# Two transformer blocks on one core: the order of weight halves, of the last differential head, of retention's sums and of the mixing sums

## The reference

```python
# first block
xn = rms_norm(h, g0);  proj = xn @ w_in          # q, k, v, forget gate, q, k, v, two gates
o_a = forgetting_attention(...)                   # 8 heads of 64
o_b = stick_breaking_attention(...)               # 8 heads of 64
mixed = (sigmoid(g_a) * (o_a @ w_o_fox) + sigmoid(g_b) * (o_b @ w_o_sb)) @ w_out
h = h + rms_norm(mixed, g1)
u = causal_depthwise_conv(rms_norm(h, g2) @ w_up) # width 2 x 2816, taps 3
h = h + rms_norm((gelu(u_gate) * u_val) @ w_down, g3)
# second block
proj = rms_norm_2(x, g_mix) @ w_in                # qa, ka, va, qr, kr, vr, gr, gate_a, gate_r
ya = rms_norm_2(diff_attention(qa, ka, va, lam), g_diff_sub) * 0.8     # 8 heads
yr = silu(gr) * rms_norm_2(retention(qr, kr, vr), g_ret_sub)           # 4 heads, two chunks of 128
x = x + (sigmoid(gate_a) * (ya @ w_branch_diff) + sigmoid(gate_r) * (yr @ w_branch_ret)) @ w_out
x = x + square(relu(rms_norm_2(x, g_mlp) @ w_ff1)) @ w_ff2
x = x + sigmoid(rms_norm_2(x, g_ple) @ w_ple_gate) * (p @ w_ple)
out = rms_norm_2(x, g_final)
```

## Time and profile before

| | us |
|---|---|
| three timed runs | 923.8, 923.9, 924.1; median 923.9 |
| the profiled run | 924.6 |
| its span, first to last instruction | 923.0 |
| busy: TensorE, VectorE, ScalarE, GpSimd | 906.6, 674.5, 475.4, 57.1 |

### The profile page before, as it was taken

One profiled execution on the slowest core, in us unless ns is written; L12 is line 12 of the kernel. 1 busy time (PEld: TensorE's weight loads), 2 busy tenths in 40 slices (PEclk: granted clock), 3 DMA queues, 4 the chain that ended last, 5 costly groups with the idle time before them and its releaser, 6 DMA issues.

```text
span 923.0 us, 17806 instructions
## 1 busy us (share of the span) xinstructions
PE 906.6 (98%) x7210; PEld 870.7 (94%) x7210; DVE 674.5 (73%) x1194; ACT 475.4 (52%) x836; POOL 57.1 (6%) x124
## 2 busy tenths in 40 slices
PE   8999999999999999999999999999999999999997
PEld 7899989999999999997999988999999999999996
DVE  7764576778877877888799886786657666666686
ACT  5355354555655455466366644564336544444466
POOL 5022000120000000000000000000102000000001
PEclk9999999999999999999999999999999999999999
DMA  8543444545456556555644464565555566666651
GB/s 313 182 151 103 136 137 120 184 138 180 145 180 193 181 175 197 181 176 156 205 138 138 131 174 130 159 187 181 183 160 182 185 197 187 185 184 183 184 159 46
DMA packets 42688, 154.71 MB, mean 168 GB/s; under 512 B 4720, under 2 KB 5232, under 8 KB 42480
## 3 DMA queue, kind: packets, MB, share of 16 engines
q1 hardware_dynamic: 42608, 153.59, 53.7%
HBM read 152.52 MB, written 1.05 MB: 166 GB/s over the span
## 4 chain that ended last, share of the span: by engine, by line
PE 86%; DVE 8%; ACT 3%; issue 2%; DMA 1%; SPq 0%; POOL 0%; DVEq 0%; ACTq 0%
PE bank L266 86%; DVE wl L1306 3%; ACT wh L863 1%; DMA raw<-in_wts 1%; DVE work L1695 0%; DVE work L1676 0%; ACT work L1116 0%; DVE wh L1302 0%; DVE tmpb L1887 0%; DVE xc L1889 0%; DVE tmpb L1612 0%; DVE work L1693 0%; DVE tmpb L1608 0%; ACT qk L1269 0%; DVE qk L1714 0%
## 5 line engine op out<-in xcount | busy, mean ns | idle before, releaser
L1306 DVE TENSOR_TENSOR wl<-raw,wh 128x1024 fp32r<-128x1024 f32 x284 | 351.7, 1247 | 109.2 <-ACT wh L863 107.4
L863 ACT ACTIVATE wh<-raw 128x1024 fp32r<-128x1024 f32 x249 | 259.9, 1052 | 163.5 <-PE bank L266 151.4
L266 PE MATMUL bank<-a2h,wh 128*128 128x256 f32 x896 | 254.2, 284 | 0.6 <-DVE wl L1306 0.6
L266 PE MATMUL bank<-a2h,wl 128*128 128x256 f32 x896 | 250.5, 280 | 0.0
L266 PE MATMUL bank<-a2l,wh 128*128 128x256 f32 x896 | 248.7, 280 | 0.0
L266 PE MATMUL bank<-a1h,wh 128*128 128x258 f32 (+1 forms) x800 | 226.8, 285 | 2.2 <-DVE wl L1306 1.2
L266 PE MATMUL bank<-a1h,wl 128*128 128x258 f32 (+1 forms) x800 | 224.0, 282 | 0.0
L266 PE MATMUL bank<-a1l,wh 128*128 128x258 f32 (+1 forms) x800 | 220.5, 282 | 0.0
L266 PEld LDWEIGHTS bank<-a2h,wh 128*128 128x128 f32 x896 | 168.9, 188 | 3.9 <-issue 2.7
L266 PEld LDWEIGHTS bank<-a2h,wl 128*128 128x128 f32 x896 | 168.8, 188 | 0.0
L266 PEld LDWEIGHTS bank<-a2l,wh 128*128 128x128 f32 x896 | 167.7, 188 | 0.3
(11 more groups left out here) (239 smaller groups left out, 990.8 us busy)
## 6 DMA issues: line engine op xcount, KB each, us to landing
raw<-in_wts SPq DMA_DIRECT2D x284, 512.0 KB, 3.7
csb<-in_cst SPq DMA_DIRECT2D x1, 1428.0 KB, 11.3
out<-va SPq DMA_DIRECT2D x2, 512.0 KB, 3.0
xc<-in_xT SPq DMA_DIRECT2D x1, 544.0 KB, 7.2
raw<-in_wts SPq DMA_DIRECT2D x2, 256.0 KB, 3.4
xc<-in_xT SPq DMA_DIRECT2D x1, 276.0 KB, 3.1
xc<-in_xT SPq DMA_DIRECT2D x1, 272.0 KB, 4.4
va<-in_pT SPq DMA_DIRECT2D x1, 256.0 KB, 3.9
```

Source lines behind the costliest of these rows:

```text
L266: return e.matmul(o, lhsT, rhs, start=start, stop=stop, skip_group_check=True)
L863: e.activation(wh[:, i % NHL, :], raw[:, i % NRAW, :], ACT.Copy).then_inc(s_hi, 1)
L1306: e.tensor_tensor(lo, src, hi.bitcast(F32), ALU.subtract).then_inc(s_lo, 1)
```

## The change

It keeps the computation and moves work, at nine places:

- A: `by_vector(1)` holds now, so VectorE makes both halves of block 1, between its low halves of tokens 2 and 3. SP waits for the first token part (`s_x[0]`) before it issues tokens(2), blocks 2 and 3 and the constants.
- B: `lo_to(B_FF + 3)` (block 60, both halves) stands ahead of the last copy of the first output projection instead of behind it.
- C: in the first feed-forward, the high halves of blocks 65 and 66 come in ScalarE's step j = 1, and those of 67 and 69 one step sooner; VectorE's low halves 65 to 67 come one eviction sooner.
- D: the high half of block 129 comes before residual 6, that of block 130 before the PLE copies.
- E: the root of the value tokens is read off the diagonal by two reductions of VectorE against the identity; TensorE's two products, their bank columns and the semaphore s_rt go. Projection tile 2 waits for the root's logarithm instead.
- F: retention's sums of heads 1 and 3 use bank 3 instead of 5, so a sum waits for the logarithm two back.
- H: at tile 20 VectorE does the pump step 41 (combination of head 7) before the eviction, and block 156 after it. The clamp and the square of head 6 come at step 43 instead of 44 and 45.
- I: in the second output projection VectorE adds the first three tiles before it makes block 209, and both engines then make one block after each activation from the second on.
- (Not timed apart from F: s_rp is waited for once more, at its third count.)

```diff
 def by_vector(i):
-    return i % 8 == 4 and i < B_GP
+    return i == 1 or i % 8 == 4 and i < B_GP
 def hid_count(i):
-    return (min(i, B_GP - 1) + 4) // 8
+    return (min(i, B_GP - 1) + 4) // 8 + (1 if i >= 1 else 0)
...
+        RET_SUM = lambda h: bank[B_S2[0] if h % 2 else B_T2][:, 0:S]
...
-                elif n == 6:
-                    e.wait_ge(s_rs, 5)
-                    for b in range(2):
-                        t = mm(bank[2][:, S + b:S + b + 1], rb[0:1, 0, b * 128:b * 128 + 128], ones[0:1, 0:1], False, True)
-                    t.then_inc(s_rt, 1)
...
             def ret_sum(h):
                 e.wait_ge(s_rqa, h + 1)
-                if h:
-                    e.wait_ge(s_rln, h)
-                mm(bank[B_T2][:, 0:S], ones, qk[:, 8 + 2 * h, 0:S], True, True).then_inc(s_rss, 1)
+                if h % 2:
+                    e.wait_ge(s_rp, 3)
+                if h >= 2:
+                    e.wait_ge(s_rln, h - 1)
+                mm(RET_SUM(h), ones, qk[:, 8 + 2 * h, 0:S], True, True).then_inc(s_rss, 1)
...
                 if t == 2:
-                    e.wait_ge(s_rtc, 1)
+                    e.wait_ge(s_ln, 5)
...
# ScalarE
-                    elif k == 4 and n == 1:
-                        hi_to(B_V2 + 4)
+                    elif k in (4, 6) and n == 1:
+                        hi_to(B_V2 + (4 if k == 4 else 5))
...
                         if j:
-                            hi_to(i + 4)
+                            hi_to({(2, 0): B_FF + 10, (3, 0): B_FF + 12}.get((j, half), i + 4))
...
+                        if (j, half) == (1, 0):
+                            hi_to(B_FF + 9)
...
             residual_hi(1, NM, L, COL_GMIX, a2h)
+            hi_to(B_V2 + 6)
             ple_out(2)
...
-                    elif a == 2:
+                    elif a == (0 if h == 6 else 2):
                         diff_square(h)
...
             hi_to(B_WOUT2 + 5)
-            for m in range(9):
-                if 3 <= m < 8:
-                    hi_to(B_WOUT2 + m + 4)
+            for m in range(8):
                 if m:
-                    e.wait_ge(s_x2, m)
-                    weighed_hi(m - 1, a1h[:, m - 1, 0:S], xk(m - 1), COL_GMLP)
-                    if m - 1 >= 5:
-                        e.wait_ge(s_sqp, Q_UP2 + m - 5)
-                    e.activation(qk[:, 2 if m == 1 else 3 + (m - 1) % 4, 0:S], xk(m - 1), ACT.Square).then_inc(s_sqa, 1)
+                    hi_to(B_WOUT2 + max(m + 4, 6))
+                e.wait_ge(s_x2, m + 1)
+                weighed_hi(m, a1h[:, m, 0:S], xk(m), COL_GMLP)
+                if m >= 5:
+                    e.wait_ge(s_sqp, Q_UP2 + m - 4)
+                e.activation(qk[:, 2 if m == 0 else 3 + m % 4, 0:S], xk(m), ACT.Square).then_inc(s_sqa, 1)
...
# VectorE
             for k in range(2, KT):
+                if k == 3:
+                    lo_to(2)
                 input_lo(k)
...
+                if m == 7:
+                    lo_to(B_FF + 3)
                 e.wait_ge(s_sqa, 4 + m + 1)
                 e.tensor_copy(qk[:, m, 0:LQ], bank[MIX_BANK[m]][:, 0:LQ]).then_inc(s_mt, 1)
...
-            lo_to(B_FF + 3)
             add_normed(0, lambda k: qk[:, k, 0:LQ], COL_G1, rb[:, 1, 0:LQ], 2, T0, L, N_UP1, COL_G2, a1h, a1l, {6: B_FF + 4})
...
-                lo_to(B_FF + 6 if n == 1 else i + 4)
+                lo_to({1: B_FF + 6, 3: B_FF + 8, 4: B_FF + 9, 5: B_FF + 10, 6: B_FF + 11, 7: B_FF + 12}.get(n, i + 4))
...
-            e.wait_ge(s_rt, 1)
-            e.tensor_copy(r_tok, bank[2][:, S:S + 2]).then_inc(s_rtc, 1)
-            e.wait_ge(s_rtc, 1)
+            e.wait_ge(s_cst, 16)
+            e.wait_ge(s_rs, 5)
+            for b in range(2):
+                e.tensor_tensor_reduce(tmpb[:, b, 0:128], rb[:, 0, b * 128:b * 128 + 128], ident, 1.0, 0.0, ALU.mult, ALU.add,
+                                       r_tok[:, b:b + 1]).then_inc(s_rtc, 1)
+            e.wait_ge(s_rtc, 2)
...
-                    elif a == 1:
+                    elif a == (0 if h == 6 else 1):
                         diff_clamp(h)
...
             def proj2(t, i, p):
-                lo_to(i + 4)
+                if t != 20:
+                    lo_to(i + 4)
                 pump2(p)
+                if t == 20:
+                    pump2(p + 1)
                 o = bank[t % 3][:, 0:S]
...
-                pump2(p + 1)
+                if t == 20:
+                    lo_to(i + 4)
+                else:
+                    pump2(p + 1)
...
# SP
             load(1)
+            e.wait_ge(s_x[0], 16)
             tokens(2, KT + 4 * L, KT + 8 * L)
```

More of the change, by code:

```diff
@@ L202, in program @@
         s_mt, s_an, s_hd = sem("s_mt"), sem("s_an"), sem("s_hd")
-        s_rt, s_rtc, s_u = sem("s_rt"), sem("s_rtc"), sem("s_u")
+        s_rtc, s_u = sem("s_rtc"), sem("s_u")
         s_cv, s_ca, s_cb, s_gl, s_gv = (sem(f"s_{n}") for n in ("cv", "ca", "cb", "gl", "gv"))
@@ L1154, in ret_root @@
                     e.wait_ge(s_rn, 2 * h - 2)
-                e.activation(r, bank[B_T2][:, 0:S], ACT.Ln, bias=eps, scale=1.0 / 256).then_inc(s_rln, 1)
+                e.activation(r, RET_SUM(h), ACT.Ln, bias=eps, scale=1.0 / 256).then_inc(s_rln, 1)
                 e.wait_ge(s_rln, h + 1)
@@ L1300, in lo_to @@
                         e.wait_ge(s_raw[i % NRAW], 16 * (i // NRAW + 1))
-                        e.wait_ge(s_blk, i - NHL + 1)
+                        if i >= NHL:
+                            e.wait_ge(s_blk, i - NHL + 1)
                         e.tensor_copy(hi, src).then_inc(s_hid, 1)
@@ L1830, in vector_engine, with mix_out @@
             mix_lo(N_MIX2, 7, a2h, a2l)
-            lo_to(B_WOUT2 + 5)
-            for m in range(9):
-                if m < 8:
-                    if m >= 3:
-                        lo_to(B_WOUT2 + m + 4)
-                    e.wait_ge(s_blk, B_WOUT2 + m + 1)
-                    e.tensor_tensor(xk(m), xk(m), bank[W_OUT_BANK(m)][:, 0:S], ALU.add).then_inc(s_x2, 1)
+            def mix_out(m):
+                e.wait_ge(s_blk, B_WOUT2 + m + 1)
+                e.tensor_tensor(xk(m), xk(m), bank[W_OUT_BANK(m)][:, 0:S], ALU.add).then_inc(s_x2, 1)
+            lo_to(B_WOUT2 + 4)
+            for m in range(3):
+                mix_out(m)
+            lo_to(B_WOUT2 + 5)
+            for m in range(8):
+                if m >= 3:
+                    mix_out(m)
                 if m:
-                    weighed_lo(N_UP2, m - 1, a1l[:, m - 1, 0:S], a1h[:, m - 1, 0:S], xk(m - 1), COL_GMLP)
+                    lo_to(B_WOUT2 + max(m + 4, 6))
+                weighed_lo(N_UP2, m, a1l[:, m, 0:S], a1h[:, m, 0:S], xk(m), COL_GMLP)
             lo_to(B_FF2 + 5)
```

## The result

The changed kernel takes 918.4 us (median of four runs, 918.0 to 918.8) where the kernel before takes 923.9: a ratio of 0.994, interval 0.9923 to 0.9957, 5.5 us less. The prediction was 916.9 with a range of 915.2 to 919.6. The profiled execution took 918.4, and its span went from 923.0 to 917.0.

The account below looks back on a forecast made before the run. TensorE was busy 906.6 of 923.0 us, so only 16.4 us of idle time could be won. Terms 1.0 + 0.3 + 1.3 + 1.5 + 0.6 + 1.6 - 0.3 + 1.0 = 7.0 took 923.9 to 916.9; range 915.2 to 919.6.

Parts of the forecast that it names:

- the forecast's 916 to 918: Whole kernel: the band of times around the forecast of 916.9 us, given a chance of 0.42.
- rival 2: Start: the held loads are late, block 2 comes 8.1 us after its issue, costing 0.5; 918.4 us, chance 0.12.
- from 6.8 to 8.5: Start: with the loads behind it held back, block 1 can land anywhere from 6.8 to 8.5 us.
- VectorE is free for it at about 7.6: Start: VectorE can convert block 1 from 7.6 us, ending at 9.55, a gain of 1.3 us.
- rival 5: Start: block 1 lands no sooner, at 8.5; only the conversions' 0.4 us is gained; 917.5 us, chance 0.10.
- What was said of block 2: Start: bandwidth, not its issue 1.2 us later, sets block 2's landing; late, its halves would be ready at 15.25.
- Rival 3: Differential heads: VectorE binds, so 2.1 us gained earlier comes back as waits at 520 to 534; 919.0 us, chance 0.14.
- The sign that I had set for it: Differential heads: waits from 500 to 534 us of over 2 us in all would show that VectorE binds.
- rival 1: Last differential head: tile 22's eviction is in time, a gain of 1.0 instead of -0.3; 915.6 us, chance 0.17.
- the right chain: Last differential head: head 6's clamp at 531.0, copy 531.8, block 158's halves 532.8 and 534.0, tile 22's eviction 534.4.
- TensorE needs that eviction for the first value block: Last differential head: TensorE comes at 533.1 and waits 1.3 us for tile 22's eviction, making the term -0.3.
- rival 4: Start: a longer stall lets the granted clock fall to 1.2 GHz, so work takes twice as long; 926 us, chance 0.02.

Follow-up runs that it names:

- the first trace of before: The first profiled execution of the unchanged kernel before; its span was 923.0 us.
- the second trace of before: The kernel before, unchanged, profiled a second time; its span was 921.6 us.

## Why the prediction was right, and where it was not

- **The sum.** The predicted parts add up to 7.0, those of the table to 5.8 for the edits, and to 6.1 with the 0.3 of C behind block 65. The median fell by 5.5. H (1.1 less than its term) and A (0.6 less) were too high, C (0.5), D and E (0.2) too low. The pace behind retention's sums, which the prediction didn't have, takes another 0.7 to 1.3; the 1.1 that the first trace of before had lost by its slow draw is no gain of the change. The time lies in the range because these misses partly cancel, and that is luck in part: 918.4 is outside the forecast's 916 to 918. It is the very number of rival 2 (block 2 late), whose sign, a wait near 13.5, is not in the trace.
- **A** was mis-sized, 1.0 for 0.4 (0.3 as the mean of seven traces against four, and 0.05 against the second trace of before alone). The failed step is "from 6.8 to 8.5": the landing was taken from the mean rate, with 1572 KB set against GB/s of thousand bytes besides (with 1610 it is 6.9), and the landing is the last engine's. "VectorE is free for it at about 7.6" failed too: in the trace of the kernel after VectorE is at the low half of tokens 2 until 8.23, since the low half of block 0's second part came at 7.05 instead of 6.52, so even a landing at 6.8 would have given 0.2 more there and not 0.9. The gain is that of the two conversions, and rival 5 (A is 0.4, 917.5 us) describes it. What was said of block 2 held: no new stall near 13.5. It was converted from 11.09 on although issued a microsecond later, where the four traces with the old start have 10.8 to 11.7.
- **B** 0.34 for 0.3, **I** 1.05 for 1.0, **F** 1.72 for 1.6 at its own place: right. The sums at 569 and 573 us run through:

```profile
569.03 1.03 PE L267 MATMUL bank<-qk,onesb 128*128 128x256 f32 x4
...
572.75 1.10 PE L267 MATMUL bank<-qk,onesb 128*128 128x256 f32 x4
```

  Each row with x4 stands for two rows x2 such as those of the earlier trace rows, with no wait between them. What the prediction didn't have is that this gain is partly given back in TensorE's pace.
- **C** 1.8 for 1.3, above its upper bound of 1.35: 1.45 at the place (alone: 1.46) and 0.3 just behind it. The stall was worth 1.37 from start to start, and no later tile is late. The 0.3 are in no term, and no run shows what they come from.
- **D and E** 2.3 for 2.1. D 1.5 (1.44 at its row, 0.1 within the next microsecond), E 0.7 where the bound was 0.64. Rival 3 fell: the lead of 5.87 at 456 is still 5.83 at 519. The sign that I had set for it, over 2 us of waits from 500 to 534, did come (2.05), from H. As a sign it was badly chosen, since it named no cause. The sign of rival 1, no new wait, didn't come.
- **H** had the right chain, each step within 0.15 us, and the right sign. The step that failed is "TensorE needs that eviction for the first value block": there is an earlier reader. TensorE comes for head 5's scaling one product sooner, and it stands behind the eviction on VectorE. The value block, forecast for 528.5 (534.4 less 5.87), starts at 529.71: 0.33 for the scaling's place behind the eviction, some 0.15 to the release, and 0.65 of products with v that no longer lie under the wait; the term is -1.4, below the bound of -1.3.
- **TensorE's busy time** fell by 1.3 instead of 0.5 against the first trace of before, and by 0.5 (905.8 to 905.3) against the second, which drew the same pace as the kernel after in the first stretch. The granted clock is 1.00 in all stretches up to 880 us, as before, so rival 4 has nothing for it.

## What to carry to other kernels

When work is moved ahead of a wait, write down for every instruction that it passes who reads its result and which bank or buffer that reader writes; the nearest such reader decides, not the one that was late before. When the wait is found, look whether the awaited instruction itself has a second queue behind its first: clearing one of two gives half (1.0 of 2.05 us here), and only both the rest. And compare a stretch without stalls by its count of matmuls as well: part of the stall that is removed can be given back there, and one trace of the kernel before may have drawn a slow stretch.

## What the hardware showed that I had not expected

TensorE, busy without a gap at a granted clock of 1.00 (its 2.4 GHz level), ran the same stream of 256-column matmuls, one weight load each, at 0.1173, 0.1187 or 0.1200 us from start to start, and held one level for some 480 matmuls; of 258-column ones mixed with these at 0.1190 or 0.1199, for some 160 us. In one place the level followed a stall ahead of the stretch (six of six, seven of seven), in the other it differed between executions of the same instructions. The stretch from 720 to 870 us ran at 0.1180 to 0.1181 in every trace, so not all stretches have such levels.
